# A Hawk/HGRN2 block on eight cores: the last two output blocks in tiles of their own, finished by halves, and other ScalarE work in the attention

## The reference

```
h = rms_norm(x, norm_g);  xa, ga, q, f, i, gb, gm = split(h @ w_in)
xa = causal_conv4(xa);  a = sigmoid(lam)^(8 r);  u = sqrt(1 - a^2) * gate_i * xa
ya = scan(h_t = a_t h_{t-1} + u_t) * silu(ga)
o  = chunked linear attention(q, 1 - f, i, log f), state 128 x 128 per head, 8 heads
yb = rms_norm(o per head) * silu(gb)
x  = x + (sigmoid(gm_a) * (ya @ proj_a) + sigmoid(gm_b) * (yb @ proj_b)) @ w_out
out = rms_norm(x) * final_norm_g
```

## Time and profile before

| | |
|---|---|
| median of 3 runs | 1404.53 us (1404.45 to 1434.55) |
| profiled execution | 1405.57 us |
| its span on the slowest core, core 1 | 1403.8 us (all cores: 1398.9 to 1403.8) |
| mean granted TensorE clock, core 1 | 0.989 |
| busy on core 1: PE, DVE, ACT, POOL | 1357.8, 1020.6, 969.3, 412.9 us |

### The profile page before, as it was taken

The page is one execution under the profiler, slowest core; times in us unless marked ns, Lnnn a source line. Parts: engine busy times, 40 slices in busy tenths (PEclk is TensorE's granted clock), DMA queues, the critical chain, the costliest instruction groups (busy, mean ns, idle before and its releaser), DMA issues.

```text
span 1403.8 us, 26365 instructions; the slowest of 8 cores (1398.9 to 1403.8 us)
## 1 busy us (share of the span) xinstructions
PE 1357.8 (97%) x7330; PEld 655.6 (47%) x7330; DVE 1020.6 (73%) x1862; ACT 969.3 (69%) x2116; POOL 412.9 (29%) x759
## 2 busy tenths in 40 slices
PE   6978999999999999999999999999999999999996
PEld 2434444544445444444445444454444544444442
DVE  5577688677788776797767887678787777687564
ACT  4688777667777676687765678756787666678741
POOL 4334444335542344332332231112312012111200
PEclk9989999999999999999999999999999999999998
DMA  9999889998999999998999758755566355544452
GB/s 172 179 201 211 134 132 160 173 180 184 199 183 162 223 198 225 196 211 195 241 239 225 204 143 240 207 150 162 176 208 166 113 187 169 149 136 135 136 187 75
DMA packets 120669, 251.47 MB, mean 179 GB/s; under 512 B 13520, under 2 KB 13648, under 8 KB 119632
## 3 DMA queue, kind: packets, MB, share of 16 engines
q0 software_dynamic: 46368, 89.94, 41.6%
q1 hardware_dynamic: 74160, 159.86, 36.7%
HBM read 301.91 MB, written 37.75 MB: 242 GB/s over the span
## 4 chain that ended last, share of the span: by engine, by line
PE 91%; ACT 3%; issue 2%; DVE 2%; DMA 1%; POOL 0%; DVEq 0%; SPq 0%; ACTq 0%; POOLq 0%
PE PS L631 68%; PE PS L639 14%; PE PS L822 1%; PE PS L784 1%; PE PS L787 1%; PE PS L682 1%; PE PS L820 1%; PE PS L679 1%; PE PS L839 1%; PE PS L805 1%; DMA GA<-xt 1%; PE PS L589 1%; ACT BB L724 0%; ACT L724 0%; PE PS L555 0%
## 5 line engine op out<-in xcount | busy, mean ns | idle before, releaser
L631 PE MATMUL PS<-HT,WS 128*128 128x512 bf16 x3584 | 836.4, 380 | 5.7 <-DVE XR L864 1.9
L631 PEld LDWEIGHTS PS<-HT,WS 128*128 128x128 bf16 x3584 | 346.8, 98 | 386.3 <-issue 13.9
L621 POOL DMA_DIRECT2D WS<-wpk x305 | 167.4, 552 | 406.2 <-PE PS L631 275.2
L668 DVE SCALAR_TENSOR_TENSOR XC<-XA,PAR,XC 128x512 f32<-128x512 f32 x192 | 141.5, 743 | 1.5 <-DVE DP L906 0.4
L631 PE MATMUL PS<-SG,WS 128*128 128x512 bf16 x512 | 115.3, 379 | 0.0
L631 PE MATMUL PS<-SGB,WS 128*128 128x512 bf16 x512 | 114.8, 379 | 0.0
L530 POOL TENSOR_TENSOR SMALL<-SMALL,NHALF 128x4 f32<-128x4 f32 (+1 forms) x102 | 107.7, 1056 | 11.9 <-PE PS L631 0.4
L788 DVE TENSOR_TENSOR ATT<-PS,MSK 128x512 bf16<-128x512 f32 x64 | 44.2, 690 | 88.7 <-PE PS L787 80.6
L529 POOL TENSOR_SCALAR SMALL<-SMALL 128x4 f32<-128x4 f32 (+1 forms) x102 | 47.5, 465 | 190.5 <-ACT JNK L827 101.7
L810 ACT ACTIVATE SBF<-ST,G 128x128 bf16<-128x128 f32 x192 | 76.1, 396 | 22.8 <-DVE ST L814 17.3
L765 ACT ACTIVATE SGB<-PS 128x512 bf16<-128x512 f32 x64 | 38.2, 597 | 72.6 <-PE PS L631 69.3
(11 more groups left out here) (131 smaller groups left out, 2351.4 us busy)
## 6 DMA issues: line engine op xcount, KB each, us to landing
WS<-wbf SPq DMA_DIRECT2D x335, 256.0 KB, 3.6
WS<-wpk POOLq DMA_DIRECT2D x305, 256.0 KB, 10.8
XR<-x SPq DMA_DIRECT2D x60, 512.0 KB, 7.7
wbf<-WS SPq DMA_DIRECT2D x80, 256.0 KB, 8.9
y<-XR SPq DMA_DIRECT2D x31, 512.0 KB, 5.2
HT<-xt POOLq DMA_DIRECT2D x7, 1024.0 KB, 12.4
WR<-wpk POOLq DMA_DIRECT2D x8, 256.0 KB, 17.7
GA<-xt SPq DMA_DIRECT2D x2, 512.0 KB, 6.8
```

Source lines behind the costliest of these rows:

```text
L621: P.emit("pool", lambda e: e.dma_start(out=W.phys[:, :], in_=dram["wpk"][k]), [], [W], dma_sem=s_ws[1], cost=560.0, nbytes=1 << 19, after= ...
L631: P.emit("pe", lambda e, k=k: e.matmul(ps.f32, W.phys[:, k * 128:(k + 1) * 128], src(k), start=(k == 0), stop=(k == 7)), [W] + src_bufs(k) ...
L668: dve(lambda e, k=k: e.scalar_tensor_tensor(C[:, :], X[:, k:k + TT], par(P_CW + 8 * k + m), C[:, :], ALU.mult, ALU.add), [bX, bC, b_PAR], ...
```

## The change

- `HOP` is raised (TensorE 240 to 270, ScalarE 150 to 220, VectorE 150 to 180, POOL 120 to 150 ns), and the lag on the same engine becomes `OWN` (ScalarE 200, VectorE 180, POOL 150 ns, before 80). Three costs of the planner are changed with it.
- Blocks (7, 2) and (7, 3) get their x rows by `x_last` into the upper and lower half of `HT[0]`, read as f32, with two buffers each, one per half. Both are finished by halves: square of a half with its sum, VectorE multiplies the half by `FNG`, and when the factor is there each half is scaled and stored. The scaling is ScalarE's, but for half 0 of block (7, 3), which is VectorE's.
- `att_b` squares `po` in one instruction of 128x512 into `JNK`, now f32, and VectorE sums it by blocks of 128.
- `lru_unit` makes M as the square of A, after L693.
- `KEEP` becomes bf16. `RAWQ` and `RAWF`, lists of units whose q or f group is copied out by VectorE first, are empty.

```diff
+LAST_X = [(NTILES - 1, 2), (NTILES - 1, 3)]
+RAWQ = []
+RAWF = []
...
-    HOP = {"pe": 240.0, "act": 150.0, "dve": 150.0, "pool": 120.0, "sp": 100.0}
+    HOP = {"pe": 270.0, "act": 220.0, "dve": 180.0, "pool": 150.0, "sp": 100.0}
+    OWN = {"pe": 0.0, "act": 200.0, "dve": 180.0, "pool": 150.0, "sp": 0.0}
...
-            return 0.0 if a.eng == "pe" else 80.0
+            return self.OWN[a.eng]
...
-        KEEP = sb("KEEP", [128, TT], F32)
+        KEEP = sb("KEEP", [128, TT], BF16)
...
-        r_JNK = ring("JNK", 1, [128, 512], BF16)
+        r_JNK = ring("JNK", 1, [128, 512], F32)
...
-            pool(lambda e: e.tensor_tensor(SMALL[:, c0:c0 + w], SMALL[:, c0:c0 + w], NHALF[:, 0:w], ALU.pow), [bs, b_NH], [bs], 60.0 + 220.0 * w, bias=bias)
+            pool(lambda e: e.tensor_tensor(SMALL[:, c0:c0 + w], SMALL[:, c0:c0 + w], NHALF[:, 0:w], ALU.pow), [bs, b_NH], [bs], 160.0 + 220.0 * w, bias=bias)
...
-            act(lambda e: e.activation(M[:, :], A[:, :], AF.Exp, scale=dp(m), bias=dp(m)), [bA, b_DP], [bM], 700.0, T_LE)
             act(lambda e: e.activation(A[:, :], A[:, :], AF.Exp, scale=dp(48 + m), bias=dp(48 + m)), [bA, b_DP], [bA], 700.0, T_LE)
+            act(lambda e: e.activation(M[:, :], A[:, :], AF.Square), [bA], [bM], 520.0)
...
-            for n in range(4):
-                act(lambda e, n=n: e.activation(J[:, CS[n]], po.f32[:, CS[n]], AF.Square, accum_out=SMALL[:, c0 + n:c0 + n + 1]), [po], [bJ, bs], 400.0, bias=AB)
+            act(lambda e: e.activation(J[:, :], po.f32, AF.Square), [po], [bJ], 520.0, bias=AB)
+            dve(lambda e: e.tensor_reduce(SMALL[:, c0:c0 + 4], J[:, :].rearrange("p (h v) -> p h v", h=4), mybir.AxisListType.X, ALU.add), [bJ], [bs], 600.0, bias=AB)
...
-                live["x", tile, j] = x_load(tile, j)
+                live["x", tile, j] = x_load(tile, j) if (tile, j) not in LAST_X else x_last(tile, j)
             X, bX, i = live["x", tile, j]
+            bX = bX[h] if (tile, j) in LAST_X else bX
...
-            if tile == NTILES - 1 and j == 3:
-                c0 = 40 + j + h
+            if (tile, j) in LAST_X:
+                c0 = 32 + 2 * (j - 2) + h
+                bm = b_SML[j - 2]
                 Q, bq, _ = r_JNK.take()
...
+                dve(lambda e: e.tensor_tensor(X[:, sl], X[:, sl], FNG[:, sl], ALU.mult), [bX, b_FNG], [bX], 615.0)
...
+                        if j == 3 and g == 0:
+                            dve(lambda e, sg=sg: e.tensor_scalar(X[:, sg], X[:, sg], r, None, ALU.mult), [bg, bm[1]], [bg], 455.0)
+                        else:
+                            act(lambda e, sg=sg: e.activation(X[:, sg], X[:, sg], AF.Copy, scale=r), [bg, bm[1]], [bg], 500.0)
...
+        def x_last(tile, j):
+            p = (tile + 1) % 2
+            g = LAST_X.index((tile, j))
+            T = HT[p][:, 4 * g:4 * g + 4, :].rearrange("p c t -> p (c t)").bitcast(F32)
+            b = bl("XL%d_" % g, 2)
+            P.emit("sp", lambda e: e.dma_start(out=T, in_=xv[tile, j]), writes=b_HT[p][4 * g:4 * g + 4] + b, dma_sem=s_xl[g], cost=450.0, nbytes=1 << 19)
+            return T, b, 0
```

More of the change, by code:

```diff
@@ L496, in _build @@
         b_TST, b_G3, b_BREF = bl("TST", 8), bl("G3", 8), bl("BREF", 8)
-        b_SMX, b_SMF, b_SMH, b_SML = Buf("SMX"), bl("SMF", 4), bl("SMH", 4), bl("SML", 2)
+        b_SMX, b_SMF, b_SMH, b_SML = Buf("SMX"), bl("SMF", 4), bl("SMH", 4), [bl("SML%d" % i, 2) for i in range(2)]
         s_c = [sem("ld_c%d" % i) for i in range(5)]
@@ L505, in _build @@
         s_ht = [sem("ld_h%d" % i) for i in range(2)]
-        s_last = [sem("st_l%d" % i) for i in range(2)]
+        s_xl = [sem("ld_xl%d" % i) for i in range(2)]
+        s_last = [sem("st_l%d" % i) for i in range(4)]
         out_ops = []
@@ L711, in q_group @@
             Q, bQ, _ = r_QT.take()
-            act(lambda e: e.activation(Q[:, :], ps.f32, AF.Silu), [ps], [bQ], 490.0, T_SILU)
+            if (tile, m) in RAWQ:
+                B, bB, _ = live["bb", tile, m] = r_BB.take()
+                dve(lambda e: e.tensor_copy(B[:, :], ps.f32), [ps], [bB], 615.0)
+                act(lambda e: e.activation(Q[:, :], B[:, :], AF.Silu), [bB], [bQ], 490.0, T_SILU)
+            else:
+                act(lambda e: e.activation(Q[:, :], ps.f32, AF.Silu), [ps], [bQ], 490.0, T_SILU)
             live["q", tile, m] = (Q, bQ)
@@ L717, in f_group @@
             S, bS, _ = r_SS.take()
-            act(lambda e: e.activation(S[:, :], ps.f32, AF.Tanh, scale=-0.5), [ps], [bS], 490.0, T_SILU)
+            if (tile, m) in RAWF:
+                dve(lambda e: e.tensor_copy(S[:, :], ps.f32), [ps], [bS], 615.0)
+                act(lambda e: e.activation(S[:, :], S[:, :], AF.Tanh, scale=-0.5), [bS], [bS], 490.0, T_SILU)
+            else:
+                act(lambda e: e.activation(S[:, :], ps.f32, AF.Tanh, scale=-0.5), [ps], [bS], 490.0, T_SILU)
             live["s", tile, m] = (S, bS)
@@ L722, in decay_unit @@
             S, bS = live["s", tile, m]
-            B, bB, _ = r_BB.take()
+            B, bB, _ = live.pop(("bb", tile, m), None) or r_BB.take()
             act(lambda e: e.activation(B[:, :], S[:, :], AF.Ln, bias=dp(8 + m), scale=dp(40 + m)), [bS, b_DP], [bB], 700.0, T_LE)
@@ L869, in wo_group @@
                 if h == 1:
[L870 to L872 removed]
+                    r, r0 = SMALL[:, c0:c0 + 1], SMALL[:, c0 - 1:c0]
+                    pool(lambda e: e.tensor_scalar(r, r, r0, None, ALU.add), bm, bm[1:], 300.0)
@@ L873, in wo_group @@
+                    pool(lambda e: e.tensor_tensor(r, r, NHALF[:, 0:1], ALU.pow), bm[1:] + [b_NH], bm[1:], 280.0)
                     for g in range(2):
-                        sg = slice(g * 512, g * 512 + 512)
-                        dve(lambda e, sg=sg: e.scalar_tensor_tensor(X[:, sg], X[:, sg], r, FNG[:, sg], ALU.mult, ALU.mult), [bX, bs[1], b_FNG], [bh[g]], 690.0)
-                        out_ops.append(P.emit("sp", lambda e, sg=sg: e.dma_start(out=yv[tile, j, :, sg], in_=X[:, sg]), [bh[g]], [], dma_sem=s_last[g], cost=450.0, nbytes=1 << 18))
+                        sg, bg = slice(512 * g, 512 * g + 512), live["x", tile, j][1][g]
+                        if j == 3 and g == 0:
+                            dve(lambda e, sg=sg: e.tensor_scalar(X[:, sg], X[:, sg], r, None, ALU.mult), [bg, bm[1]], [bg], 455.0)
+                        else:
+                            act(lambda e, sg=sg: e.activation(X[:, sg], X[:, sg], AF.Copy, scale=r), [bg, bm[1]], [bg], 500.0)
+                        out_ops.append(P.emit("sp", lambda e, sg=sg: e.dma_start(out=yv[tile, j, :, sg], in_=X[:, sg]), [bg], [], dma_sem=s_last[2 * (j - 2) + g], cost=450.0, nbytes=1 << 18))
```

9 lines of the change are left out of this document (4 added, 5 removed).

## The result

The changed kernel takes 1396.87 us (median of 5 runs, 1395.58 to 1398.71), the one before 1404.74 us on the same chip. The ratio is 0.9944 [0.9929, 0.9958]: 7.9 us less, where 6.3 were predicted. The profiled execution took 1398.71 us, with core 6 the slowest (1397.2 us).

What follows compares the result with a forecast made beforehand. TensorE's own work was taken to bound the middle, leaving start and tail to move the time. Tail 5.1 + squares 1.2 + decay 0 + figures 0 = 6.3 us off the median of 1404.53: 1398.2 us, range 1387 to 1405.

Steps and rivals of the forecast that it cites:

- if these holes have gone, moved or multiplied: Start: sign that the prediction is wrong, about TensorE's holes with slow clock stretches near 93 and 138 us.
- Part 1: Tail, last two blocks: no wait for x, separate half buffers and side-by-side scalings give 2.99 + 1.62 + 0.48 = 5.1 us.
- taken as 0: Tail: ScalarE's two scalings of block (7, 2) before the last square cost 0 to 0.7 us, counted as 0.
- Part 2: Attention: one square with VectorE's sum replaces four; 1.2 us gained at the start, nothing in the middle.
- In the middle stage this is worth 0: From 180 to 1376 us: ScalarE's 75 us relief and VectorE's 44 us of sums gain nothing.
- Part 3: Recurrence's decay made by a square: batch 2.95 us before, 2.96 after; taken as 0, bounds -0.8 to +0.4 us.
- Part 4: Planner figures and types, all engines: queues may be arranged anew; taken as 0 between two ends of about equal weight.
- The hole is ScalarE's queue: Start: TensorE's 6.45 us idle at the first slow stretch is put on ScalarE, busy 9.08 of 10.20 us there.
- (a): Start: rival that the lighter ScalarE and the new order close the holes, giving 1389.7 us; chance 0.20.
- (b): First tiles: rival that the new order opens a hole of its own, giving 1409.8 us; chance 0.16.
- (c): Start: rival that VectorE is late or holds ScalarE through JNK, at most 5.4 us, giving 1403.6; chance 0.08.
- (d): Tail: rival that loads are placed late or scalings collide, gaining only 2 us, giving 1401.3; chance 0.06.

Runs made afterwards that it cites:

- run 3: Kernel before with only one 128x512 attention square plus VectorE's sum (KEEP bf16, JNK f32), old planner figures: ratio 1.0082, slower by 11.5 us.
- run 2: Kernel before with only the planner's figures changed (HOP, OWN and two costs): ratio 0.9986, 2.0 us less.
- run 7: Kernel before with the attention's light squares and the planner's figures, without the decay's square and the last blocks: ratio 0.9948, 1397.4 us.
- run 9: Changed kernel in its own order, with four squares and sums on ScalarE and a four-column copy replacing VectorE's sum: ratio 1.0054.
- run 4: The changed kernel measured again beside the first three runs on their chip, against the kernel before: ratio 0.9935.
- run 6: Changed kernel with the planner's old figures (HOP, OWN, two costs): ratio 1.0051 to the kernel before.
- run 5: Kernel before, its order kept on every engine, with the one attention square and VectorE's sum placed late: ratio 1.0053, slowest core 1415.6 us for 1403.1.
- run 12: Kernel before, its order kept, with the one attention square and VectorE's sum right behind it: no ratio, slowest core 1415.8 us for 1402.8.
- run 8: Changed kernel with the last half scaled and multiplied by FNG in one VectorE instruction, block (7, 2)'s second scaling on VectorE: ratio 0.9911.

## Why the prediction was right, and where not

**The total** came out right, 7.9 us for 6.3, but by luck: 1.4 us from the tail where 5.1 stood, some 6 from the start and order where 1.2 stood. Two errors of opposite sign made up for each other. The prediction also named a sign of being wrong, "if these holes have gone, moved or multiplied", and it came: the first hole is three waits now, and both slow stretches stand 3.5 us earlier.

**Part 1, the tail.** Right: the loads go out at 1222.7 us, far ahead; the last L864 (now L879) is 2.14 us behind the group, for 2.07; the scalings run side by side and the second store goes 1.03 us behind the factor, for 1.0. Mis-sized on core 1: 3.2 us for 5.1. The terms were these. The square starts 1.70 us behind the start of the last L879 instead of 0.84: +0.86. The scaling of block (7, 2) on ScalarE had been "taken as 0". From the square to the scaling are 2.46 us instead of 2.02: +0.44. This term was taken from the trace of before, without asking what runs beside it now. From the second store to the end are 4.8 us instead of 4.3: +0.5; the stores land 2.0 to 2.3 us behind their issue, before 2.1, so it lies in what follows, and no run tells why. With the 0.07 and 0.03 of above that is the 1.9 us; the second store goes 7.3 us behind the group's start, for 5.9. And core 1 was the worst case: its tail before was 13.87, the median 12.4, so that the time of the slowest core gains less.

**Part 2, the squares.** The sum takes 0.678 us, as taken from L696, and the square 0.58. VectorE's 1056.8 us for 1065 and ScalarE's 934.7 for 894 miss, ScalarE's by half of the saving: L827's instructions cover 92.4 us before and L840's 37.5 after, but run 3, which changes only them, saves 32 us and not 55, since they ran partly over the end of their neighbours on ScalarE. The step that failed is "In the middle stage this is worth 0". It is worth +14 us of run-up with the old figures and the order made from them (run 3) and -5 with the new ones (runs 2 and 7). That ScalarE is "an engine that isn't the bound" was true by busy time and misleading, since every engine works in an order fixed beforehand: run 9 puts 30 us of work back on ScalarE in the new order and is 14 us slower.

**Part 3, the decay.** The batch takes 3.02 us per unit (from 87.30 to 90.32), for 2.96. Zero was right (run 7).

**Part 4, the figures.** "I take 0": alone, 2 us (run 2); with the squares, 19 (runs 3, 4 and 6). The bounds had been made for the figures by themselves. That parts 2 and 4 act on each other had no term: they stood at 1.2 and 0 us by themselves, and this is the step that failed. What the runs show in its place is that the two together give 17 to 19 us more than the sum of each alone (runs 2, 3 and 4).

**"The hole is ScalarE's queue".** ScalarE was 89% busy there, but run 5 frees it earlier and leaves the hole. What stands between is VectorE's queue behind the product that waits for POOL, 8.1 us in runs 5 and 12 as before; in the changed kernel the scans stand ahead of it and it is 2.5. That this reorder is what shortens the hole is read from the two orders; no run changed it alone. And the holes are not what the figures win: the waits for `KT` are as short in the slow runs 3 and 6.

**The rivals.** (a) came nearest in mechanism: the waits for `KT` became shorter by 2.6 us but did not close, and the stretches at the lower clock stayed, though shorter on most cores. (b) did not come; runs 3 and 6 do end slower by a new order, but not by a hole of the first tiles. (c): one new wait of 2.2 us, for the product that has the sum and POOL ahead of it, is of its kind, but more is won beside it; `JNK` held ScalarE long only in run 5. The Trainium skill, page "VectorE: DVE Perf Modes", section "Rules for kernel authors", says to expect the lowest rate of `tensor_reduce` on a hot path and to consider restructuring. The rate is as said: the 691 ns worked out from that page's formula, which it gives for an f32 `tensor_tensor`, an estimate, agree with the 678 measured. The advice had no say in the changed kernel, which has 64 such sums and is faster; whether they make runs 5 and 12 slow is open. (d) is close to what happened: the tail gave 1.4 us at the slowest core, in part by scalings that collide.

**What stays open.** Why the one square with VectorE's sum costs 13 us in the order of before (runs 5 and 12). VectorE's added 0.68 us in each unit is the rival left, and was not tested alone. In run 5 TensorE of core 1 is idle 7.4 us more (2.0 at the start, 5.4 in the middle), of 10.7 us of longer run-up; the waits for `KT` (+1.6), `SBF` (+2.5) and `ONB` (+2.1) hold 6 of it. Of the changed kernel's 7.2 us on core 1, 4.0 are idle time and 1.7 the stretch at half clock that is gone; the rest isn't placed. Last, why core 6 waited for weights in the profile; in the changed kernel's second profile no core stands out so.

## What to carry to other kernels

Where all engines work in an order computed beforehand, work moved from one engine with time to spare to another can make the kernel slower: the order is packed to the planner's durations. So change work and figures together, and set the figures from the trace (how long a round from engine to engine takes); here figures below the measured round and figures 1.4 times as long both lost. Test such parts in pairs, not only one by one, and one side at a time where work moves from one engine to another. In a tail, look at what stands ahead of the last square on its engine and what runs beside each step of the last chain.

## What the runs showed of the hardware

POOL's addition of one column took 0.77 us while VectorE multiplied two operands from SBUF (1386.17 to 1386.86; POOL's 1386.24 to 1387.01, 0.15 us after VectorE's end), and 0.28 us in run 8 without that neighbour. The Trainium skill, page "SBUF — State Buffer", section "Who interferes with whom", has a rule for this: a VectorE instruction with two inputs from SBUF contends with a GpSimd instruction that reads SBUF; the trace agrees. The other small additions of this tail that ran into such a VectorE instruction took 0.61 to 0.90 us.

Reading ScalarE's accumulator took 0.20 us (mean) behind the squares of L827, four times in a unit, 51.2 us in the whole span by the groups of L827.
